# The first pair's rows as products with one-hot columns stationary, then turned like every other pair

## The chip, the cores and the metric

The kernel runs on 1 core of a Trainium2 chip. The metric is device time in microseconds (us), the median of several executions. In the trace and below, PE is TensorE (matrix products; PEld its loads of the stationary operand), DVE is VectorE, ACT is ScalarE, POOL is GpSimd and SP the engine that issues most transfers.

## What is computed

One step of a decoder trunk of two layers, on 512 prompt rows and 32 sample rows of width 1024, all float32. Each layer is a mixer (gated linear attention and a state-space scan in layer 0, pooling and block-sparse attention in layer 1), a residual with layer norm, a mixture of 32 experts (4 groups of 8, each row goes to one group and to two experts in it), and another residual with layer norm. The change lies between the first norm and the experts, in both layers:

```python
def _hier_moe(x, w_coarse, b_coarse, w_fine, b_fine, w_gate_up, w_down):
    xt = x.reshape(bsz * t, d)
    lc = xt @ w_coarse + b_coarse                    # 4 groups
    grp = argmax(lc); p_grp = softmax(lc)[grp]
    lf = einsum('nd,gde->nge', xt, w_fine) + b_fine  # 8 experts of each group
    top_v, top_i = lax.top_k(lf[grp], 2)
    gates = one_hot(top_i) * softmax(top_v) * p_grp
    for g in range(N_GROUPS):
        hg, hu = split(einsum('nd,edf->nef', xt, w_gate_up[g]), 2)
        out = out + einsum('nef,efd->nd', silu(hg) * hu * gate_g, w_down[g])
```

## The kernel before, in words

The 544 rows are five tiles in the order ORDER: the 32 sample rows first (i = 0), then four tiles of 128 prompt rows (i = 1 to 4). All five tiles stay on the chip in X.

A stage called settle (`settle_parts`) makes, tile by tile, the output projection of the mixer (`project`, L1378: products of 128x512 into the three banks `pp`, which are `ahead`), the residual and statistics (DVE, L1525 to L1530), the router's logits (`flip` L1394, `score` L1406) and the choice of experts (`choose`). The norm is applied to X by ACT (L1730) and then scale and bias by DVE (`affine`, L1564 and L1565), which says `final` when a tile is finished; SP then stores the tile to `token_rows` in memory (L1351).

The experts stage (`expert_parts`) goes through the 32 experts in 16 pairs. A pair takes 128 slots, 64 for each of its two experts. For pairs 1 to 15 POOL gathers the rows from `token_rows` into one of two tiles `xg` (L1279), PE turns them (`x_T`, 8 transposes, L1835), ACT and DVE copy them to `xT` (L1912), and then come `gate_up` in two halves (L1850), the hidden layer, and `down` (L1874). Rows over 64 for an expert go to extra pairs; one such pair runs in each layer.

The weights of a pair are 6 transfers of 1 MB: four for gate and up (`load_up`, L1254), two for down (`load_down`, L1260). They go round a ring of three places. Pairs 0 and 1 are loaded early. In `sync`, pair 2's four `up` transfers are issued after the last projection, then the store of the last tile, which waits for `final`, and then pair 2's two `down` transfers: the second of these overwrites `E.wd[-1]`, where the scale and bias (`gb`) lie until the last tile's `affine` is done. From pair 3 on, `Experts.load` waits for PE: the first half of `up` for the first half of gate_up three pairs back (`half_used`), the second half for its second half, `down` for the down products three pairs back. So pair 3's first transfers are released by the end of the first pair's gate_up, half 0 (L2005).

The first pair does not gather. DVE makes one-hot columns G (`heat`, L1621; 128 columns for each tile, which say what slot a row takes), and PE's `pick(i)` sums X-transposed times G over the five tiles straight into the turned form: 8 products for a tile, each with 128 columns of X (every eighth element of a row) stationary and 128 columns of G moving (L1436). ACT copies the sum to `xT` (L1734), and `first.gate_up` runs.

Beside it DVE works out where each row goes: `position` (L1611 to L1614) for a tile from PE's `count` (L1416), `start_of` (L1603), the tiles of an expert (L1659, from PE's `totals`, L1427), PE's prefix sums `placed` (L1477, L1479), and the chain from L1671 to the one-hots L1684 and L1687 (`destined`, `onehots`), from which PE makes the tables of rows (L1488, L1493).

Of the kernel before, what the change touches and what calls it, by code (L numbers as in the profile page):

```python
# [91 lines left out]
class Count:  # L92


    def __init__(self, eng, sem):
        self.eng, self.sem, self.n = eng, sem, 0
# [1129 lines left out]
class Experts:  # L1226
# [29 lines left out]

    def load_down(self, eng, i):
        for a in range(2):
            row = (self.l * NE + 2 * i + a) * 128
            eng.dma_start(self.wd[2 * (i % self.RING) + a][:, :], self.w_dn[row:row + 128, :])\  # L1260
               .then_inc(self.down_in[i % self.RING], 16)
# [22 lines left out]
def settle_parts(nc, s, place, C, X, lng, lnb, ln_T, mixT, w_dram, l, w_router, b_router, lg, xT, rows, E, back, done, ahead, first, old=None):  # L1284
# [24 lines left out]
    slots = place("slots", [128, 5, 2])  # L1309
    G = E.xg[0][:, 0:640].rearrange("p (t n) -> p t n", t=5)  # L1310

# [16 lines left out]
    x_in = [s.sem(f"x_in{i}") for i in range(5)]  # L1328
    hot, tables = s.sem("hot"), s.sem("tables")
    xt, x0, sl, hr = first.picked, first.x0, first.sl, first.hr  # L1330

    def sync(sp):
        sp.dma_start(wr[:, :, :], w_router[l]).then_inc(router_in, 16)
        sp.dma_start(gbT[:, :, :], ln_T).then_inc(router_in, 16)
        sp.dma_start(br[:, :], b_router[l].partition_broadcast(128)).then_inc(router_in, 16)
        if back:
            for i, (t, P) in enumerate(ORDER):
                sp.dma_start(X[:P, t, :], back(t)).then_inc(x_in[t], 16)
                if i == 0:
                    for p, got in ((slice(0, 32), old_in), (slice(32, 128), rest_in)):  # L1340
                        for a in range(2):
                            sp.dma_start(E.xg[a][p, :], old[a].partition_broadcast(p.stop - p.start)).then_inc(got, 16)
        sp.dma_start(gb[:, 0, :], lng.partition_broadcast(128)).then_inc(gb_in, 16)
        sp.dma_start(gb[:, 1, :], lnb.partition_broadcast(128)).then_inc(gb_in, 16)
        E.fill(sp, range(E.RING - 1))
        for i, (t, P) in enumerate(ORDER):
            if i == 4:
                sp.wait_ge(summed, 10)
                E.load_up(sp, E.RING - 1)
            sp.wait_ge(final, i + 1)  # L1350
            sp.dma_start(rows[tok0(t):tok0(t) + P, :], X[:P, t, :]).then_inc(stored, 16)  # L1351
        E.load_down(sp, E.RING - 1)

    def gpsimd(pool):
        if old:
            pool.wait_ge(old_used, 1)
        for x in E.xg:
            nc.gpsimd.memset(x[:, :], 0.0).then_inc(blank, 1)  # L1358
        pool.wait_ge(blank, 2)
        pool.wait_ge(told, 1)  # L1360
        pool.wait_ge(stored, 16 * 5)
        E.rows(pool, rows, 1, s.kept[f"e{l}_rows1"])
        pool.wait_ge(tables, 1)

    def tensor(pe):
# [57 lines left out]
        def totals():  # L1423
            pe.wait_ge(logit_c, 4)
            pe.wait_ge(assigned, 5)
            for i in range(5):
                last = nc.tensor.matmul(pm[1][0:32, 0:8], A12[:, i, :], C("ones")[:, 0:8], start=(i == 0), stop=(i == 4))  # L1427
            last.then_inc(counted, 1)

        def pick(i):  # L1430
            t, P = ORDER[i]
            pe.wait_ge(hot, i + 1)
            pe.wait_ge(final, i + 1)
            rows_of = X[:P, t, :].rearrange("r (p j) -> r j p", j=KD)
            for j in range(KD):
                last = nc.tensor.matmul(pt[j // 4][:, (j % 4) * 128:(j % 4) * 128 + 128], rows_of[:, j, :], G[:P, i, :],  # L1436
                                        start=(i == 0 and j % 4 == 0), stop=(i == 4), skip_group_check=True)
            if i == 4:
                last.then_inc(xt, 1)

# [5 lines left out]
        for i in range(1, 5):  # L1446
# [14 lines left out]
            if i < 4:  # L1461
# [9 lines left out]
        pick(0)  # L1471
        pick(1)
        totals()
        count(4)
        pick(2)
        pe.wait_ge(tiled, 1)
        nc.tensor.matmul(pm[0][:, 0:32], tilesT[:, 0:1].to_broadcast([32, 128]), C("before")[0:32, 0:32],  # L1477
                         start=True, stop=True)
        nc.tensor.matmul(pm[0][:, 32:64], tilesT[:, 0:1].to_broadcast([32, 128]), C("tri_p")[0:32, 0:32],  # L1479
                         start=True, stop=True).then_inc(placed, 1)  # L1480
        pick(3)
        pick(4)
        first.gate_up(pe, 0)
# [13 lines left out]
    def vector(dve):  # L1497
# [58 lines left out]

        def affine(i):
            t, P = ORDER[i]
            if i == 0:
                dve.wait_ge(gb_in, 32)  # L1560
            for h in range(2):
                x = X[:P, t, 512 * h:512 * h + 512]
                dve.wait_ge(normed, 2 * i + h + 1)
                c.step(V.tensor_tensor(x, x, gb[:P, 0, 512 * h:512 * h + 512], ALU.mult))  # L1564
                last = V.tensor_tensor(x, x, gb[:P, 1, 512 * h:512 * h + 512], ALU.add)  # L1565
            last.then_inc(final, 1)

# [49 lines left out]
        def heat(i):  # L1617
            dve.wait_ge(positioned, i + 1)
            if i == 0:
                dve.wait_ge(blank, 2)  # L1620
            V.tensor_tensor(G[:, i, :].rearrange("p (e n) -> p e n", e=2), slots[:, i, :].unsqueeze(2).to_broadcast([128, 2, 64]),  # L1621
                            C("iota")[:, 1:65].unsqueeze(1).to_broadcast([128, 2, 64]), ALU.is_equal).then_inc(hot, 1)
# [32 lines left out]
        position(3)  # L1655
        heat(3)
        start_of(4)
        dve.wait_ge(counted, 1)
        c.step(V.tensor_tensor(cmpT[:, :], pm[1][0:32, 0:8], C("m64")[0:32, :], ALU.is_gt))  # L1659
        V.tensor_reduce(tilesT[:, :], cmpT[:, :], AX.X, ALU.add).then_inc(tiled, 1)  # L1660
        position(4)
        heat(4)
        affine(4)
        c.wait()
        r10, b10 = rsel[:, :, :].rearrange("p k t -> p (k t)"), bsel[:, :, :].rearrange("p k t -> p (k t)")
# [53 lines left out]
    def scalar(act):  # L1719
        for i, (t, P) in enumerate(ORDER):  # L1720
# [7 lines left out]
            for h in range(2):  # L1728
                x = X[:P, t, 512 * h:512 * h + 512]
                nc.scalar.activation(x, x, ACT.Identity, bias=nmr[:P, t:t + 1], scale=rstd[:P, t:t + 1])\  # L1730
                  .then_inc(normed, 1)
        act.wait_ge(xt, 1)
        for h in range(2):
# [10 lines left out]
def expert_parts(nc, s, C, E, xT, xd, yd, first, px, py, Y, y_in):  # L1744
# [13 lines left out]
    all_landed = s.sem("all_landed")  # L1758
    xt, gh, gu, sl, hr = first.picked, first.gh, first.gu, first.sl, first.hr
    xta, xtd, ht, htc, dn, ya, ydv = (s.sem(x) for x in ("x_act", "x_dve", "h_T", "h_copied", "down", "y_act", "y_dve"))  # L1760
# [231 lines left out]
class FirstPair:  # L1992


    def __init__(self, nc, se, E, xT, pg, ph):
        self.nc, self.E, self.xT, self.pg, self.ph = nc, E, xT, pg, ph
        self.picked, self.x0, self.gh, self.gu, self.sl, self.hr = (se.sem(x) for x in (
            "x_T", "x_first", "gate_up_half", "gate_up", "silu", "hidden"))

    def gate_up(self, pe, h):  # L2000
# [18 lines left out]
def settle_and_experts(nc, l, C, X, lng, lnb, ln_T, mixT, w_dram, w_router, b_router, lg, xT, xd, yd, E, back, done, ahead, old, y_in):  # L2019


    with Scope(nc, f"n{l}0") as s, Scope(nc, f"e{l}") as se:
# [13 lines left out]

        first = FirstPair(nc, se, E, xT, ahead[0:2], ahead[2])
        (sync1, pool1, pe1, dve1, act1), px, py = settle_parts(nc, s, place, C, X, lng, lnb, ln_T, mixT, w_dram, l, w_router,
# [915 lines left out]
```

## Time and profile before

| | us |
|---|---|
| three runs | 1339.84, 1342.57, 1347.92 |
| median | 1342.57 |
| time of the profiled execution | 1343.1 |
| its span | 1341.2 |
| mean granted TensorE clock | 0.922 |
| PE busy | 1139.0 (85%) |
| DVE busy | 488.2 (36%) |
| ACT busy | 253.7 (19%) |
| memory traffic, mean over the span | 279 GB/s |

The time holds 1.9 us more than the span (1343.1 - 1341.2), which lie around the program. A product of float32 stands in the trace as two records, with two loads of the stationary operand; a transpose stands as one. PEclk is the granted clock as a share of 2.4 GHz: 1.00 is 2.4 GHz, 0.50 is 1.2 GHz, a value between is a stretch with both.

### The profile page before, as it was taken

How to read it: one execution, taken by the hardware profiler on the slowest of the kernel's cores; microseconds unless marked ns; L12 is line 12 of the kernel's file. 1: busy time of each engine (PE TensorE's matmuls, PEld its weight loads, DVE VectorE, ACT ScalarE, POOL GpSimd, SP SyncE). 2: the span in 40 equal slices, each digit the busy share in tenths (PEclk: the TensorE clock that was granted, in tenths of full speed). 3: DMA queues.
4: the chain of work that ended last, by engine and by line, in shares of the span. 5: the costliest groups of instructions: out<-in, count | busy, mean ns of one | idle time of the engine just before them, and what ended most of it. 6: DMA issues, size and time to landing. Idle time of an engine off the chain costs nothing. (4 is left out here: it accounts for less than half of the span.)

```text
span 1341.2 us, 15442 instructions
## 1 busy us (share of the span) xinstructions
PE 1139.0 (85%) x5825; PEld 591.5 (44%) x5825; DVE 488.2 (36%) x1338; ACT 253.7 (19%) x548; POOL 186.0 (14%) x182
## 2 busy tenths in 40 slices
PE   7999999969999977884689998987999999778552
PEld 5874666635753322221334345544457433223110
DVE  2614755556631111113411324654775211111008
ACT  0311222411111111112411213241111111111011
POOL 0000000000011111102533542220000211111112
PEclk9999998989889988897789999998998999889885
DMA  7430301173369999995866998793916999999914
GB/s 266 159 107 1 130 1 63 72 286 162 155 259 413 419 421 420 420 386 199 318 205 244 396 360 323 304 342 106 420 50 228 358 418 419 421 420 421 387 66 159
DMA packets 84453, 358.90 MB, mean 268 GB/s; under 512 B 13828, under 2 KB 18053, under 8 KB 54422
## 3 DMA queue, kind: packets, MB, share of 16 engines
q1 hardware_dynamic: 62774, 279.63, 52.7%
q0 software_dynamic: 19520, 74.01, 14.4%
q10 hardware_dynamic: 2080, 4.19, 0.8%
q8 instruction: 50, 0.82, 0.2%
q14 instruction: 29, 0.24, 0.0%
HBM read 342.82 MB, written 31.16 MB: 279 GB/s over the span
## 5 line engine op out<-in xcount | busy, mean ns | idle before, releaser
L1850 PE MATMUL ahead_psum<-m_wg,top_xT 128*64 128x512 f32 x672 | 165.6, 641 | 44.6 <-DMA m_wg<-in_moe_w_gate_up 43.6
L1874 PE MATMUL n_psum_m<-m_wd,top_xT 128*64 128x512 f32 x528 | 123.9, 612 | 5.5 <-DMA m_wd<-in_moe_w_down 3.4
L1378 PE MATMUL ahead_psum<-top_wide,top_xT 128*128 128x512 f32 x240 | 112.4, 616 | 8.6 <-DVE top_X L1527 8.6
L1850 PEld LDWEIGHTS ahead_psum<-m_wg,top_xT 128*64 128x64 f32 x672 | 50.8, 147 | 152.7 <-issue 98.3
L1850 PE MATMUL ahead_psum<-top_wide,top_xT 128*64 128x512 f32 x320 | 80.1, 648 | 19.9 <-DMA top_wide<-in_moe_w_gate_up 19.9
L1912 DVE COPY top_xT<-n_psum_t 128x512 f32<-128x512 f32 x31 | 21.4, 692 | 188.3 <-PE n_psum_t L1835 188.3
L2251 PE MATMUL cd_psum_ab<-top_wide,top_xT 128*128 128x512 f32 x192 | 87.9, 611 | 0.1
L1279 POOL DMA_INDIRECT m_xg<-token_rows,m_tokof x31 | 31.5, 1018 | 373.8 <-PE n_psum_t L1835 198.7
L1921 DVE TENSOR_SCALAR e_Y<-n_psum_m,m_share 128x512 f32<-128x512 f32 x33 | 24.8, 751 | 129.7 <-PE n_psum_m L1874 129.7
L2095 POOL DMA_INDIRECT cd_kv<-in_cache_kT,top_kpages x64 | 60.6, 947 | 78.8 <-PE cd_psum_d L2293 51.0
L1378 PEld LDWEIGHTS ahead_psum<-top_wide,top_xT 128*128 128x128 f32 x240 | 45.3, 197 | 57.4 <-issue 57.3
L1874 PEld LDWEIGHTS n_psum_m<-m_wd,top_xT 128*64 128x64 f32 x528 | 36.3, 140 | 68.7 <-issue 61.3
L1783 POOL DMA_INDIRECT expert_rows<-e_Y,m_dest x33 | 32.7, 992 | 188.1 <-DVE e_Y L1921 187.2
L2251 PEld LDWEIGHTS cd_psum_ab<-top_wide,top_xT 128*128 128x128 f32 x192 | 36.5, 195 | 49.1 <-issue 49.0
L588 PE MATMUL ab_psum<-top_wide,top_xT 128*128 128x512 f32 x128 | 56.9, 597 | 0.0
L1850 PEld LDWEIGHTS ahead_psum<-top_wide,top_xT 128*64 128x64 f32 x320 | 24.3, 148 | 73.1 <-issue 47.9
L1358 POOL MEMSET m_xg<- 128x1024 f32 x4 | 3.7, 949 | 380.5 <-POOLq L144 275.2
L1965 DVE TENSOR_TENSOR top_xT<-top_xT,ahead_psum 128x256 f32<-128x256 f32 x31 | 13.1, 421 | 103.4 <-ACT top_xT L1934 103.4
L1929 ACT ACTIVATE top_xT<-ahead_psum 128x256 f32<-128x256 f32 x33 | 12.6, 383 | 193.5 <-PE ahead_psum L1861 193.5
L1920 ACT ACTIVATE e_Y<-n_psum_m,m_share 128x512 f32<-128x512 f32 x33 | 22.7, 687 | 109.1 <-PE n_psum_m L1874 109.1
L2104 POOL DMA_INDIRECT cd_kv<-in_cache_v,top_pages x32 | 30.1, 940 | 78.9 <-PE cd_psum_e L2334 62.6
L1436 PE MATMUL n_psum_t<-m_xg,top_X 128*128 128x128 f32 (+1 forms) x160 | 40.4, 430 | 0.0
(488 smaller groups left out, 1668.4 us busy)
## 6 DMA issues: line engine op xcount, KB each, us to landing
m_wg<-in_moe_w_gate_up SPq DMA_DIRECT2D x88, 1024.0 KB, 26.3
m_wd<-in_moe_w_down SPq DMA_DIRECT2D x64, 1024.0 KB
top_wide<-in_moe_w_gate_up SPq DMA_DIRECT2D x40, 1024.0 KB, 25.4
cd_kv<-in_cache_kT SPq DMA_DIRECT2D x64, 256.0 KB
m_wg<-expert_rows SPq DMA_DIRECT2D x16, 512.0 KB, 5.8
ab_w<-in_ab_w_in SPq DMA_DIRECT2D x2, 2048.0 KB, 11.7
top_wide<-in_ab_w_in SPq DMA_DIRECT2D x2, 2048.0 KB, 7.7
top_wide<-in_ab_w_out SPq DMA_DIRECT2D x2, 2048.0 KB, 8.6
```

The lines of the kernel that those rows point to most:

```text
L588: last = mm(out[:, :], xT[:, k, tok0(t):tok0(t) + 128], w[i][:, k, :], start=(k == 0), stop=(k == KD - 1))
L1279: pool.indirect_dma_start(out=self.xg[i % 2][:, :], out_offset=None, in_=xd, in_offset=bass.IndirectOffsetOnAxis(ap=self.tokof[:, i:i + 1] ...
L1378: last = nc.tensor.matmul(pp[(2 * i + h) % 3][:P, :], mixT[:, k, tok0(t):tok0(t) + P], w[h][:, k, :], start=(k == 0), stop=(k == KD - 1))
L1436: last = nc.tensor.matmul(pt[j // 4][:, (j % 4) * 128:(j % 4) * 128 + 128], rows_of[:, j, :], G[:P, i, :], start=(i == 0 and j % 4 == 0), ...
L1783: nc.gpsimd.indirect_dma_start(out=yd, in_=Y[i % 2][:, :], in_offset=None, out_offset=bass.IndirectOffsetOnAxis(ap=E.dest[:, i:i + 1], axi ...
L1850: last = nc.tensor.matmul(pg[i % 2][64 * a:64 * a + 64, :], xgT[i % 2][:, j, 64 * a:64 * a + 64], wg[2 * (i % NR) + a][:, j * 512:(j + 1) ...
L1874: last = nc.tensor.matmul(py[n2][64 * a:64 * a + 64, :], hT[:, j, 64 * a:64 * a + 64], wd[2 * (i % NR) + a][:, j * D + n2 * 512:j * D + (n ...
L1920: ins = nc.scalar.activation(dst, py[half][:, :], ACT.Copy, scale=share) if half == 0 else \
L1921: nc.vector.tensor_scalar(dst, py[half][:, :], share, None, ALU.mult)
L2095: pool.indirect_dma_start(out=self.slots[slot][:, b, 512 * j:512 * j + 512], out_offset=None, in_=self.k_rows, in_offset=bass.IndirectOffs ...
L2104: pool.indirect_dma_start(out=self.slots[slot][:, b, :], out_offset=None, in_=self.v_rows, in_offset=bass.IndirectOffsetOnAxis(ap=self.pag ...
L2251: last = nc.tensor.matmul(out[:, :], xT[:, k, tok0(t):tok0(t) + 128], w[r][:, k, :], start=(k == 0), stop=(k == KD - 1))
```

## The change

`pick` makes, for each tile, two products of 128x512 with G stationary and X moving, into the banks `pp[1]` and `pp[2]`: the first pair's rows as plain rows. ACT copies these to `xg[0]`, and 8 transposes (`first.x_T`) turn them, as for other pairs. G moves to `xg[1]`, and only `xg[1]` is blanked by POOL. The last tile's `affine` is done in halves with `position(4)` and `heat(4)` between them, `final` counts halves, `start_of(4)` and L1659 stand behind the second half, and PE's `count(4)` stands ahead of `totals`, and `placed` behind the last `pick`. One of pair 2's two `down` transfers is issued ahead of the last tile's store.

```diff
-    def load_down(self, eng, i):
-        for a in range(2):
+    def load_down(self, eng, i, experts=(0, 1)):
+        for a in experts:
@@
-    G = E.xg[0][:, 0:640].rearrange("p (t n) -> p t n", t=5)
+    G = E.xg[1][:, 0:640].rearrange("p (t n) -> p t n", t=5)
@@ sync
                 E.load_up(sp, E.RING - 1)
-            sp.wait_ge(final, i + 1)
+                E.load_down(sp, E.RING - 1, (0,))
+            sp.wait_ge(final, 2 * i + 2)
             sp.dma_start(rows[tok0(t):tok0(t) + P, :], X[:P, t, :]).then_inc(stored, 16)
-        E.load_down(sp, E.RING - 1)
+        E.load_down(sp, E.RING - 1, (1,))
@@ gpsimd
-        for x in E.xg:
-            nc.gpsimd.memset(x[:, :], 0.0).then_inc(blank, 1)
-        pool.wait_ge(blank, 2)
+        nc.gpsimd.memset(E.xg[1][:, :], 0.0).then_inc(blank, 1)
         pool.wait_ge(told, 1)
         pool.wait_ge(stored, 16 * 5)
+        pool.wait_ge(xt, 1)
         E.rows(pool, rows, 1, s.kept[f"e{l}_rows1"])
@@ tensor
         def pick(i):
             t, P = ORDER[i]
             pe.wait_ge(hot, i + 1)
-            pe.wait_ge(final, i + 1)
-            rows_of = X[:P, t, :].rearrange("r (p j) -> r j p", j=KD)
-            for j in range(KD):
-                last = nc.tensor.matmul(pt[j // 4][:, (j % 4) * 128:(j % 4) * 128 + 128], rows_of[:, j, :], G[:P, i, :],
-                                        start=(i == 0 and j % 4 == 0), stop=(i == 4), skip_group_check=True)
-            if i == 4:
-                last.then_inc(xt, 1)
+            for h in range(2):
+                pe.wait_ge(final, 2 * i + h + 1)
+                last = nc.tensor.matmul(pp[1 + h][:, :], G[:P, i, :], X[:P, t, 512 * h:512 * h + 512], start=(i == 0), stop=(i == 4))
+                if i == 4:
+                    last.then_inc(picked, 1)
@@
         pick(0)
         pick(1)
+        count(4)
         totals()
-        count(4)
         pick(2)
+        pick(3)
+        pick(4)
         pe.wait_ge(tiled, 1)
...
-        pick(3)
-        pick(4)
+        first.x_T(pe, rows_out, pt)
         first.gate_up(pe, 0)
@@ vector
-        def affine(i):
+        def affine(i, halves=(0, 1)):
...
-            for h in range(2):
+            for h in halves:
...
-                last = V.tensor_tensor(x, x, gb[:P, 1, 512 * h:512 * h + 512], ALU.add)
-            last.then_inc(final, 1)
+                V.tensor_tensor(x, x, gb[:P, 1, 512 * h:512 * h + 512], ALU.add).then_inc(final, 1)
@@
         heat(3)
+        affine(4, (0,))
+        position(4)
+        heat(4)
+        affine(4, (1,))
+        c.wait()
         start_of(4)
         dve.wait_ge(counted, 1)
...
-        position(4)
-        heat(4)
-        affine(4)
-        c.wait()
+        dve.wait_ge(positioned, 5)
@@ scalar
+        for h in range(2):
+            act.wait_ge(picked, h + 1)
+            nc.scalar.activation(E.xg[0][:, 512 * h:512 * h + 512], pp[1 + h][:, :], ACT.Copy).then_inc(rows_out, 1)
         act.wait_ge(xt, 1)
@@ class FirstPair
+    def x_T(self, pe, rows_out, px):
+        pe.wait_ge(rows_out, 2)
+        xv = self.E.xg[0][:, :].rearrange("r (p j) -> r j p", j=KD)
+        for j in range(KD):
+            last = self.nc.tensor.transpose(px[j // 4][:, (j % 4) * 128:(j % 4) * 128 + 128], xv[:, j, :], self.C("ident"))
+        last.then_inc(self.turned, 1)
```

PE, layer 0, from the last logits to the first pair's gate_up, before (the row of one program line with its count; L1436 is `pick`, L2005 gate_up):

```order
L1406 MATMUL n_psum_m<-e_Y,top_xT 128x36 x4
L1436 MATMUL n_psum_t<-m_xg,top_X 128x128 x16
L1427 MATMUL n_psum_m<-top_consts,e_Y 32x8 x5
L1416 MATMUL n_psum_r<-e_Y,top_consts 128x32
L1436 MATMUL n_psum_t<-m_xg,top_X 128x128 x8
L1477 MATMUL n_psum_m<-top_consts,e_Y 128x32
L1479 MATMUL n_psum_m<-top_consts,e_Y 128x32
L1436 MATMUL n_psum_t<-m_xg,top_X 128x128 x16
L2005 MATMUL ahead_psum<-m_wg,top_xT 64x512 x8
```

The same place in the changed kernel (L1435 is `pick`, L2007 the transposes of `first.x_T`, L2015 gate_up):

```order
L1406 MATMUL n_psum_m<-e_Y,top_xT 128x36 x4
L1435 MATMUL ahead_psum<-top_X,m_xg 128x512 x4
L1416 MATMUL n_psum_r<-e_Y,top_consts 128x32
L1427 MATMUL n_psum_m<-top_consts,e_Y 32x8 x5
L1435 MATMUL ahead_psum<-top_X,m_xg 128x512 x6
L1477 MATMUL n_psum_m<-top_consts,e_Y 128x32
L1479 MATMUL n_psum_m<-top_consts,e_Y 128x32
L2007 MATMUL n_psum_t<-top_consts,m_xg 128x128 x8
L2015 MATMUL ahead_psum<-m_wg,top_xT 64x512 x8
```

40 products of 128 columns became 10 of 512, `placed` (L1477, L1479) moved behind all of them, and 8 transposes came in between.

DVE, layer 0, behind `heat(3)` (the first row), before (L1564, L1565 are `affine`, L1603 `start_of`, L1611 `position`, L1666 the next chain):

```order
L1621 TENSOR_TENSOR m_xg<-e_Y,top_consts 128x128
L1603 TENSOR_TENSOR e_Y<-e_Y,top_consts 128x64
L1604 TENSOR_REDUCE e_Y<-e_Y 128x2
L1659 TENSOR_TENSOR e_Y<-n_psum_m,top_consts 32x8
L1660 TENSOR_REDUCE e_Y<-e_Y 32x1
L1611 TENSOR_TENSOR e_Y<-e_Y,n_psum_r 128x64
L1613 TENSOR_REDUCE e_Y<-e_Y 128x2
L1614 SCALAR_TENSOR_TENSOR e_Y<-n_psum_r,e_Y 128x2
L1621 TENSOR_TENSOR m_xg<-e_Y,top_consts 128x128
L1564 TENSOR_TENSOR top_X<-top_X,m_wd 128x512
L1565 TENSOR_TENSOR top_X<-top_X,m_wd 128x512
```

And now (L1563 and L1564 are `affine`, L1601 `start_of`, L1609 `position`, L1619 `heat`):

```order
L1619 TENSOR_TENSOR m_xg<-e_Y,top_consts 128x128
L1563 TENSOR_TENSOR top_X<-top_X,m_wd 128x512
L1564 TENSOR_TENSOR top_X<-top_X,m_wd 128x512
L1609 TENSOR_TENSOR e_Y<-e_Y,n_psum_r 128x64
L1611 TENSOR_REDUCE e_Y<-e_Y 128x2
L1612 SCALAR_TENSOR_TENSOR e_Y<-n_psum_r,e_Y 128x2
L1619 TENSOR_TENSOR m_xg<-e_Y,top_consts 128x128
L1563 TENSOR_TENSOR top_X<-top_X,m_wd 128x512
L1564 TENSOR_TENSOR top_X<-top_X,m_wd 128x512
L1601 TENSOR_TENSOR e_Y<-e_Y,top_consts 128x64
L1602 TENSOR_REDUCE e_Y<-e_Y 128x2
L1662 TENSOR_TENSOR e_Y<-n_psum_m,top_consts 32x8
```

The first half of the last tile's scale and bias moved ahead of its one-hot, and the count of tiles (now L1662) behind the second half.

## Rows read from the trace of the kernel before

**Rows 1.** The page: busy share of the DMA engines in 40 slices of the span

```profile
DMA  7430301173369999995866998793916999999914
```

**Rows 2.** Windows, layer 0: length, PE, PEld, DVE, ACT, POOL busy, PEclk, DMA share, GB/s

```profile
350.60:362.00 11.40, 10.31 (x49) 9.71 (x50) 6.80 (x32) 2.21 (x4) 0.00 (x0) 0.74 0.92 357
362.00:367.00 5.00, 5.00 (x29) 4.86 (x28) 3.88 (x13) 0.00 (x0) 0.00 (x0) 0.58 0.07 30
367.00:372.40 5.40, 5.40 (x25) 5.36 (x25) 4.70 (x14) 0.00 (x0) 0.00 (x0) 0.75 0.88 326
372.40:381.60 9.20, 8.42 (x31) 4.74 (x29) 1.20 (x9) 3.88 (x5) 0.00 (x0) 0.78 0.22 94
381.60:402.00 20.40, 20.12 (x110) 11.05 (x112) 6.52 (x21) 2.65 (x5) 3.16 (x3) 0.92 0.86 313
402.00:420.00 18.00, 18.00 (x89) 6.45 (x85) 2.29 (x4) 2.43 (x5) 4.00 (x4) 1.00 1.01 402
```

**Rows 3.** What SP issues in layer 0: start, length of the issuing, line

```profile
350.62 2.01 SPq L1254 DMA_DIRECT2D top_wide<-in_moe_w_gate_up  x4
...
367.18 1.26 SPq L1260 DMA_DIRECT2D m_wd<-in_moe_w_down  x2
381.62 6.74 SPq L1254 DMA_DIRECT2D m_wg<-in_moe_w_gate_up  x4
```

**Rows 4.** PE in order of time, layer 0: start, length, records, idle before

```profile
336.38 3.60 PE L1378 MATMUL ahead_psum<-top_wide,top_xT 128*128 128x512 f32 x8
...
353.73 8.29 PE L1436 MATMUL n_psum_t<-m_xg,top_X 32*128 32x128 f32 x32
...
363.03 4.04 PE L1436 MATMUL n_psum_t<-m_xg,top_X 128*128 128x128 f32 x16
...
367.56 7.90 PE L1436 MATMUL n_psum_t<-m_xg,top_X 128*128 128x128 f32 x32
376.24 5.35 PE L2005 MATMUL ahead_psum<-m_wg,top_xT 128*64 128x512 f32 x16 [0.78 <-ACT top_xT L1734]
381.52 2.41 PE L1488 MATMUL n_psum_m<-top_xT 128*128 128x24 f32 x20
...
390.77 1.97 PE L1835 MATMUL n_psum_t<-top_consts,m_xg 128*128 128x128 f32 x8
```

**Rows 5.** PE in order of time, layer 1

```profile
1010.28 8.19 PE L1436 MATMUL n_psum_t<-m_xg,top_X 32*128 32x128 f32 x32
...
1019.06 4.05 PE L1436 MATMUL n_psum_t<-m_xg,top_X 128*128 128x128 f32 x16
...
1032.27 3.65 PE L2005 MATMUL ahead_psum<-m_wg,top_xT 128*64 128x512 f32 x16 [0.78 <-ACT top_xT L1734]
1035.86 2.41 PE L1488 MATMUL n_psum_m<-top_xT 128*128 128x24 f32 x20
...
1063.14 1.06 PE L1835 MATMUL n_psum_t<-top_consts,m_xg 128*128 128x128 f32 x8
```

**Rows 6.** Loads of the stationary operand, and a product, by line: ns least/median/greatest

```profile
L1378 PEld LDWEIGHTS ahead_psum<-top_wide,top_xT x240: 186/190/337, 282.9 to 1005.9; 128*128 128x128 f32 x120
L1378 PE MATMUL ahead_psum<-top_wide,top_xT x240: 592/592/1192, 282.9 to 1006.3; 128*128 128x512 f32 x120
L1436 PEld LDWEIGHTS n_psum_t<-m_xg,top_X x160: 307/335/338, 353.7 to 1031.0; 128*128 128x128 f32 x128, 32*128 32x128 f32 x32
```

**Rows 7.** DVE in order of time, layer 0

```profile
358.24 0.29 DVE L1621 TENSOR_TENSOR m_xg<-e_Y,top_consts 128x128 f32<-128x128 f32 x1
...
364.04 0.69 DVE L1564 TENSOR_TENSOR top_X<-top_X,m_wd 128x512 f32<-128x512 f32 x1
...
367.74 0.19 DVE L1671 TENSOR_SCALAR e_Y<-n_psum_m 128x32 f32<-128x32 f32 x1 [0.40 <-PE n_psum_m L1479]
...
372.29 0.42 DVE L1687 TENSOR_TENSOR top_xT<-e_Y,top_consts 128x256 f32<-128x256 f32 x1
```

**Rows 8.** ACT in order of time, layer 0

```profile
375.49 1.09 ACT L1734 ACTIVATE top_xT<-n_psum_t 128x512 f32<-128x512 f32 x2 [20.74 <-PE n_psum_t L1436]
```

More of the change, by code:

```diff
@@ L1328, in settle_parts @@
     x_in = [s.sem(f"x_in{i}") for i in range(5)]
-    hot, tables = s.sem("hot"), s.sem("tables")
-    xt, x0, sl, hr = first.picked, first.x0, first.sl, first.hr
+    hot, tables, picked, rows_out = (s.sem(x) for x in ("hot", "tables", "picked", "rows_out"))
+    xt, x0, sl, hr = first.turned, first.x0, first.sl, first.hr
     def sync(sp):
@@ L1619, in heat @@
             if i == 0:
-                dve.wait_ge(blank, 2)
+                dve.wait_ge(blank, 1)
             V.tensor_tensor(G[:, i, :].rearrange("p (e n) -> p e n", e=2), slots[:, i, :].unsqueeze(2).to_broadcast([128, 2, 64]),
@@ L1758, in expert_parts @@
     all_landed = s.sem("all_landed")
-    xt, gh, gu, sl, hr = first.picked, first.gh, first.gu, first.sl, first.hr
+    xt, gh, gu, sl, hr = first.turned, first.gh, first.gu, first.sl, first.hr
     xta, xtd, ht, htc, dn, ya, ydv = (s.sem(x) for x in ("x_act", "x_dve", "h_T", "h_copied", "down", "y_act", "y_dve"))
@@ L1992, with __init__ @@
 class FirstPair:
-    def __init__(self, nc, se, E, xT, pg, ph):
-        self.nc, self.E, self.xT, self.pg, self.ph = nc, E, xT, pg, ph
-        self.picked, self.x0, self.gh, self.gu, self.sl, self.hr = (se.sem(x) for x in (
+    def __init__(self, nc, se, C, E, xT, pg, ph):
+        self.nc, self.C, self.E, self.xT, self.pg, self.ph = nc, C, E, xT, pg, ph
+        self.turned, self.x0, self.gh, self.gu, self.sl, self.hr = (se.sem(x) for x in (
             "x_T", "x_first", "gate_up_half", "gate_up", "silu", "hidden"))
+    def x_T(self, pe, rows_out, px):
[4 more added lines that the diff above has]
+        last.then_inc(self.turned, 1)
     def gate_up(self, pe, h):
@@ L2035, in place @@
             return v
-        first = FirstPair(nc, se, E, xT, ahead[0:2], ahead[2])
+        first = FirstPair(nc, se, C, E, xT, ahead[0:2], ahead[2])
         (sync1, pool1, pe1, dve1, act1), px, py = settle_parts(nc, s, place, C, X, lng, lnb, ln_T, mixT, w_dram, l, w_router,
```

## The prediction

> **What bounds the kernel now.** I read the page first, for where the memory is busy. The row of the DMA engines has two long stretches of 9s, slices 13 to 18 and 32 to 37: there the experts' weights stream in, and ahead of each is a weaker stretch [rows 1]. Then the windows of layer 0 say what goes on at that edge. From 402 us on the DMA engines are full (share 1.01) and nothing PE does can shorten the stream; but from 362 to 367 us their share is 0.07, from 372.4 to 381.6 us 0.22, and from 381.6 to 402 us 0.86, while PE is busy nearly all the time [rows 2]. So the stream's end is set by when it starts and by how much idle time lies in front of it. What starts it is the row of SP: after pair 2's loads (350.62 and 367.18 us) nothing is issued until 381.62 us [rows 3], and that is 0.1 us behind the start of PE's L1488 at 381.52 us, that is, the end of the first pair's gate_up, half 0 [rows 4]. PE sets it: `pick` runs from 353.73 us, gate_up begins at 376.24 us [rows 4]. Layer 1 is the same, with pick from 1010.28, gate_up from 1032.27 and its end at 1035.86 us [rows 5]. The question is how much earlier gate_up's half 0 ends.
>
> **What the old pick costs.** 8.29 us for two tiles, 4.04 for one, 7.90 for two: 20.2 us a layer [rows 4]. A tile has 16 records, so 253 ns for each; the load of the stationary operand is 335 ns in the middle (every eighth element of a row), where projections with contiguous columns have 190 ns [rows 6], and PEld is busy 4.86 of the 5.00 us from 362 to 367 [rows 2]. So loads bound it. That a tile took 4.04 us in a stretch at mean clock 0.58 and 3.95 at 0.75 [rows 2, 4] agrees.
>
> **What the new one costs.** A tile is two products of 128x512 with contiguous columns of G stationary. The nearest row is the projection: 8 records, 4 products, in 3.60 us [rows 4]. The last record lasts 592 ns to its end [rows 6], the other seven start (3.60-0.59)/7 = 0.43 us apart, so a product in a chain costs 0.86 us; 3.60/4 = 0.90 is the upper end. Ten make 8.6 us (to 9.0). The 592 ns are the same under all records but the slow ones, and a slow record takes up to 1192 [rows 6].
>
> **The new chain to gate_up, layer 0.** Picks 0 and 1 start at 353.73 and take 3.44, to 357.17. `count(4)` then waits for `position(3)`, just ahead of the one-hot of tile 3 at 358.24 [rows 7]; so it starts at 358.25, a wait of 1.1 that the old picks hid. `count` and `totals` take 0.6 (1010.28 + 8.19 to 1019.06 in layer 1 [rows 5]): 358.85. Picks 2 to 4, 5.16: 364.0. Does DVE keep up? Behind 358.24+0.29 it has now half an `affine` (two of 0.69 [rows 7], ACT's norm being done at 375.49-20.74 = 354.75, when its idle time began [rows 8]), position and one-hot of tile 4 (0.8, from the same pattern ahead of 364.04), and the second half: hot 5 at about 360.7, the last `final` at 362.0, the tile count at 362.9. Pick 4 starts at 362.3, its second product at 363.1: none of these is late, the nearest with 1 us in hand. `placed` takes 0.7 until DVE goes on (0.6 on PE); DVE resumes at 364.7, where it was 367.74 [rows 7].
>
> The relay is what the change adds on this path. ACT's copy of half 0 lies under the last product. That of half 1 starts some 0.2 behind it, at 364.2, and takes 0.6 (two of 128x512 from PSUM take 1.09, the second overlapping [rows 8]): 364.8. PE starts the transposes at 364.95. Eight cost 1.06 at full clock [rows 5] and 1.97 in the row at 390.77 [rows 4]; I take 1.06, since all that precedes is dense 512-column work like the projection. From the last transpose to gate_up there are two halves of the same ACT copy, of which the first is waited for, 0.78 as now [rows 4]. Gate_up starts at 366.8, 9.4 us before 376.24. It took 5.35 in layer 0 and 3.65 in layer 1 [rows 4, 5]: the first at a mixed clock (0.78 from 372.4 to 381.6 [rows 2]) after 22 us of load-bound picks. Behind dense products I expect 3.65. Then half 0 ends at 370.4, where it was 381.52: **11.1 us**. With the old 5.35 it would be 9.4.
>
> **Layer 1.** Its pick starts 656.55 us behind layer 0's, and what precedes is the same, so gate_up starts at 1023.35, 8.9 before 1032.27, and with 3.65 as before ends 8.9 us earlier: **8.9 us** [rows 5].
>
> On the transposes the Trainium skill speaks otherwise: "TensorE: Matmul & The Clock Gate", Part 4, says that the full clock does not engage for transposes. The trace differs: eight took 1.06 us in the stretches at 1.00 [rows 2, 5]. By that page they would take 1.97, and the sum would be 1.8 us less, 1325.
>
> **What else moves, and its cover.** PE's L1488 waits for `destined` and the one-hots. They ended at 372.71 [rows 7], 8.8 us ahead; the DVE chain moves only 3.0 us, to 369.7, so the cover shrinks to 0.7 us in each layer. If DVE is later than I have it, L1488 and all behind it (half 1, and the gather of pair 1) wait for the excess. The waits for the ring: pair 2's loads begin at 350.62 as before. Six of 1.05 MB at the 402 GB/s of 402 to 420 us [rows 2] take 15.6 us, the store of half a MB 1.3, so they are in by 368, ahead of 370.4. The `down` half that is issued early fills the idle stretch from 362 us; the other half waits behind the last store, now at 362.0 instead of 366.8. It is costed at nothing, as is the later store behind 1 MB, since the gather needs it only after the tables (L1488 plus 3 us). Without the early half the loads would end near 368 all the same; the cost would still be nothing. Bounds: 0 to 1 us. One blanking less on POOL and the gather's wait for the transposes (366 us, gather wanted at 374): nothing, in both directions. The old stores and copies need nothing else.
>
> **Can the stream use the whole gain?** Idle DMA time between 350.6 and 402 is 0.9+4.7+0.6+7.2+2.9 = 16.3 us [rows 2], more than 11.1. Behind the release the chain (gate_up 1, tables, gather, down of pair 0) keeps its order and lengths, so the 2.9 us there stay, and the full stretch starts and ends earlier by the same amount. What follows the experts waits for them.
>
> **Sum.** 11.1 + 8.9 = 20.0 us. Against the profiled execution's 1343.1 that is **1323.1 us**; the median is 0.5 lower than it, so I say 1323.
>
> **Rivals.**
> (1) *DVE sets the tables.* If the split `affine` and waits leave the one-hots 3 us behind my 369.7, 2.3 us a layer are lost for all but the first release: 1323 + 4.6 = 1328. For it: the cover is 0.7. Against: every DVE term is a measured row.
> (2) *Picks at the lower clock.* Stretches around the old picks are at 0.58 to 0.78 [rows 2]. If the new ones run at 1.2 GHz, each product takes 1.71 (twice 0.86, for it would be bound by columns): 8.6 more, less the 1.1 wait that they would fill, 7.5 a layer: 1338, no change that can be told. Against: the projection of the same form ran at 0.86 just before, and picks follow it with 512 columns, not 128.
> (3) *Slower: the lower clock holds from the picks to the end of gate_up's half 1.* Full-clock work of 8.6 + 1.0 + 3.6 + 3.6 = 16.8 a layer runs twice as long, less 1.1: 15.7, in both 31.4 against the gain of 20.0: 1354. It decides once more than 20 us of such work in both layers are at 1.2 GHz. For it: two waits for ACT of 0.4 and 0.8 us stand ahead of gate_up; against: the old chain had the second of these and layer 1 ran 3.65 behind it.
> (4) *The change doesn't do what it says:* a product with G and X stays as slow as a tile of 4.04 for a reason that is not the load. Then picks end at 375, the relay of 2.8 comes on top, gate_up starts 1.6 to 2 us later than before: 1343 to 1347. Against: 335 ns against 190 [rows 6].
>
> On the loads, the same page (LDWEIGHTS, "loading the stationary operand") gives a time that goes by columns, 107 ns for 128, whatever the rows. By that, an estimate, 16 loads would be 1.7 us, the load would not be what the old tile's 4.04 came from, and rival 4 would hold. The trace differs, with 335 and 190 ns for 128 columns each, and the measurement decides.
>
> **How the numbers follow.** Forecast 0.75, rival 1 0.12, rival 2 0.06, rival 3 0.03, rival 4 0.04. The forecast's own spread: layer 0's and 1's gate_up at a mixed clock, +1.7 each, transposes at 1.97, +1.8, products at 0.90, +0.8, loads late, +1: to 1330. Downward, what follows (transposes of pair 1 at 390.77 took 1.97, also slow) may gain 1 to 3 us from a better clock: 1320. The three runs of before lie from 2.7 below to 5.4 above their median, so a median of the new can be off by 2 to 4. With rival 1 inside, the range is 1317 to 1333. It leaves rivals 2 to 4 out. A median of this kernel tells 0.5% (6.7 us) from no change: faster than that is forecast and rival 1, 0.87; within it rivals 2 and 4, 0.09; slower 0.04 (rival 3 and a bad end of 4).
>
> **What would show it.** Right: L1435 in 4 and 6 products at 0.86 each; a wait of about 1 us ahead of L1416; ACT's L1734 in the place given and L2007 about 1 us long; gate_up from 366.8 and, in layer 1, from 1023.35-11.1 = 1012.3, SP's releases at 370.5 and 1015.9; DMA share over 0.5 in the stretch 370 to 380. Wrong: PEclk near 0.5 during L1435 or L2015, PE waiting for L1684 or L1687 ahead of L1487, PE waiting for DMA in the first gate_ups, or a stream whose first full stretch starts earlier while its end stays.

## The result

The changed kernel took 1327.57 us (median of 4 runs, 1320.55 to 1333.42) where the kernel before, in 4 runs, took 1341.20: a ratio of 0.9892, 95% interval 0.9859 to 0.9924. In a second series it was 0.9869 (0.9844 to 0.9894). So it is 1.1 to 1.3% faster, some 14 to 18 us. The forecast was 1323 in a range of 1317 to 1333: the direction and the mechanism held, and the gain was 12 to 32% smaller than the 20.0 us forecast. The profiled execution of the changed kernel is its slowest of the first series, 1333.42 us; its span is 1331.6.

PE in order of time in layer 0 of the changed kernel (start, length, records):

```profile
354.46 6.18 PE L1435 MATMUL ahead_psum<-top_X,m_xg 32*128 32x512 f32 x8
360.43 0.47 PE L1416 MATMUL n_psum_r<-e_Y,top_consts 128*128 128x32 f32 x2
360.84 0.70 PE L1427 MATMUL n_psum_m<-top_consts,e_Y 128*32 128x8 f32 x10
361.47 7.68 PE L1435 MATMUL ahead_psum<-top_X,m_xg 128*128 128x512 f32 x12
...
369.84 1.16 PE L2007 MATMUL n_psum_t<-top_consts,m_xg 128*128 128x128 f32 x8
371.78 3.65 PE L2015 MATMUL ahead_psum<-m_wg,top_xT 128*64 128x512 f32 x16 [0.78 <-ACT top_xT L1737]
375.36 2.41 PE L1487 MATMUL n_psum_m<-top_xT 128*128 128x24 f32 x20
```

and in layer 1:

```profile
1006.39 6.17 PE L1435 MATMUL ahead_psum<-top_X,m_xg 32*128 32x512 f32 x8
...
1013.39 7.69 PE L1435 MATMUL ahead_psum<-top_X,m_xg 128*128 128x512 f32 x12
...
1023.71 3.65 PE L2015 MATMUL ahead_psum<-m_wg,top_xT 128*64 128x512 f32 x16 [0.78 <-ACT top_xT L1737]
1027.29 2.41 PE L1487 MATMUL n_psum_m<-top_xT 128*128 128x24 f32 x20
```

I count the stretch from the start of the first pick to the start of the tables' products (L1488 before, L1487 now), which start 0.1 us ahead of the release of pair 3's loads, and call it the chain. The release in layer 0, SP's row:

```profile
375.46 6.74 SPq L1254 DMA_DIRECT2D m_wg<-in_moe_w_gate_up  x4
```

The chain was 27.8 us in layer 0 and 25.6 in layer 1 [rows 4, 5]; it is 20.9 in both now. That is 6.9 and 4.7 us less, 11.6 together, where 20.0 were forecast. One thing in the chain is far from the forecast: the ten products take 6.0 + 7.6 us instead of 3.4 + 5.2. That hides the wait of 1.1 us that was forecast ahead of L1416, and `count` and `totals` take 1.0 instead of 0.6; the rest has the length of the forecast. The clock says why. Windows of the changed kernel, layer 0 (columns as in [rows 2]):

```profile
350.00:354.40 4.40, 3.30 (x20) 2.12 (x18) 2.38 (x7) 1.12 (x3) 0.00 (x0) 1.00 0.46 127
354.40:357.00 2.60, 2.60 (x7) 0.82 (x6) 2.05 (x12) 1.09 (x2) 0.00 (x0) 0.77 1.01 419
357.00:360.40 3.40, 3.40 (x4) 1.37 (x5) 3.12 (x14) 0.00 (x0) 0.00 (x0) 0.50 1.01 422
360.40:363.00 2.60, 2.60 (x15) 1.79 (x14) 2.14 (x7) 0.00 (x0) 0.00 (x0) 0.50 1.02 429
363.00:366.00 3.00, 3.00 (x5) 1.11 (x4) 1.29 (x9) 0.00 (x0) 0.00 (x0) 0.50 0.98 406
366.00:369.00 3.00, 3.00 (x8) 1.12 (x6) 0.00 (x0) 0.60 (x1) 0.00 (x0) 0.99 1.04 425
369.00:371.80 2.80, 1.89 (x15) 1.54 (x14) 1.81 (x6) 1.36 (x3) 0.00 (x0) 1.00 0.13 56
371.80:375.40 3.60, 3.60 (x17) 1.25 (x17) 3.43 (x13) 1.60 (x2) 0.00 (x0) 1.00 0.00 0
```

From about 356 to 366 us the granted clock was 1.2 GHz, as it was at the same place before [rows 2], only that there the picks did not feel it. It is full again for the transposes and gate_up, so layer 0's gate_up took the 3.65 us of the forecast, against 5.35 in the profile of the kernel before. The DMA engines, idle for some 7 us ahead of the old release (0.78 of 9.2 us [rows 2]), are still idle for 6.

### The profile page after: what moved, and what is told of

The parts are those of the page before. It is cut to its first block and busy times, and to the rows that moved or that the text cites. A ratio compares the mean times of both kernels' runs of the same rounds, so it can differ in the third digit from the quotient of the medians.

```text
span 1331.6 us, 15236 instructions
## 1 busy us (share of the span) xinstructions
PE 1131.4 (85%) x5721; PEld 566.9 (43%) x5721; DVE 487.7 (37%) x1338; ACT 256.3 (19%) x552; POOL 187.5 (14%) x180
## 5 line engine op out<-in xcount | busy, mean ns | idle before, releaser
L2261 PE MATMUL cd_psum_ab<-top_wide,top_xT 128*128 128x512 f32 x192 | 85.2, 597 | 0.0
L1723 ACT ACTIVATE top_xT<-n_psum_t 128x512 f32<-128x512 f32 (+1 forms) x20 | 10.2, 532 | 140.9 <-PE n_psum_t L1394 140.9
## 6 DMA issues: line engine op xcount, KB each, us to landing
top_wide<-in_moe_w_gate_up SPq DMA_DIRECT2D x40, 1024.0 KB, 24.3
```

The source lines that it names most:

```text
L2261: last = nc.tensor.matmul(out[:, :], xT[:, k, tok0(t):tok0(t) + 128], w[r][:, k, :], start=(k == 0), stop=(k == KD - 1))
```

## The experiments

Each kernel was timed in a series beside the kernel before, on the same chip. Ratios are to that. The series are three: one with `fill`, `fill_pick2`, `form_only` and `order_only`, one with `delay`, `down_late`, `before_contig` and `before_fill`, and one with the changed kernel again, both `fill` kernels again and `wait_more`. Only the last of them has the changed kernel in it.

**One part of the change at a time.** `form_only` undoes all of the change but the new picks, the copy and the transposes, and what these need (G's new place, the one blanking, `final` in halves):

```diff
@@ vector
         heat(3)
-        affine(4, (0,))
-        position(4)
-        heat(4)
-        affine(4, (1,))
-        c.wait()
         start_of(4)
...
+        position(4)
+        heat(4)
+        affine(4)
+        c.wait()
@@ tensor
-        count(4)
         totals()
+        count(4)
         pick(2)
-        pick(3)
-        pick(4)
         pe.wait_ge(tiled, 1)
...
+        pick(3)
+        pick(4)
@@ sync
-                E.load_down(sp, E.RING - 1, (0,))
...
-        E.load_down(sp, E.RING - 1, (1,))
+        E.load_down(sp, E.RING - 1)
```

> The new form of the picks with copy and transposes, but the old order on DVE and PE (scale and bias of the last tile behind its one-hot and in one piece, totals ahead of count(4), placed ahead of pick 3) and both down transfers behind the last store. If the new form alone carries the gain: 21 to 22 us from first pick to release, 1327 to 1330. If the last tile's scale and bias must come earlier for it to pay: DVE ends them some 3 us later than in the changed kernel, at 12.8 us behind the first pick instead of 8.7, and with picks 3 and 4 then done by 14 to 15 us nothing waits for more than 0.5 us at the low clock; so I expect at most 1 us a layer lost, under 1330.

It took 1326.17 us, ratio 0.9864 (0.9831 to 0.9897): all of the gain, as far as these intervals can tell. Its chains were 18.5 and 20.0 us, shorter than the 21 to 22 that I expected, because the clock fell for a shorter time. The wait that I expected to be under 0.5 us is 0.69: PE waits so long for ACT's second copy, since `placed` no longer fills that gap.

`order_only` is the other half: the new order, the split scale and bias, and the early down transfer, with the old picks.

```diff
-            for h in range(2):
-                pe.wait_ge(final, 2 * i + h + 1)
-                last = nc.tensor.matmul(pp[1 + h][:, :], G[:P, i, :], X[:P, t, 512 * h:512 * h + 512], ...)
...
+            pe.wait_ge(final, 2 * i + 2)
+            rows_of = X[:P, t, :].rearrange("r (p j) -> r j p", j=KD)
+            for j in range(KD):
+                last = nc.tensor.matmul(pt[j // 4][...], rows_of[:, j, :], G[:P, i, :], ...)
...
-        first.x_T(pe, rows_out, pt)
@@ scalar
-        for h in range(2):
-            act.wait_ge(picked, h + 1)
-            nc.scalar.activation(E.xg[0][:, 512 * h:512 * h + 512], pp[1 + h][:, :], ACT.Copy).then_inc(rows_out, 1)
```

> The old form of the picks (8 products with strided X stationary for a tile, straight into the turned form, no copy and no extra transposes) with the new order, the split scale and bias and the early down transfer. Theory: the loads of X bound the picks, so the new order gives nothing: 20.2 us of picks a layer, 25.7 to 27.9 us from first pick to release as before, 1340 to 1342. If the order carries part of the gain, it would be below 1337.

1340.44 us, ratio 0.9986 (0.9962 to 1.0011), chains 26.2 and 26.2, the release here 0.9 us ahead of the tables. The time shows no gain, and there is a flaw that the changed kernel barely avoids: with `placed` behind all picks DVE's one-hots are late, and the tables wait for them. PE in layer 0 of `order_only`:

```profile
374.52 3.65 PE L2013 MATMUL ahead_psum<-m_wg,top_xT 128*64 128x512 f32 x16 [0.22 <-ACT top_xT L1735]
379.10 2.41 PE L1488 MATMUL n_psum_m<-top_xT 128*128 128x24 f32 x20 [0.92 <-DVE top_xT L1687]
```

In the changed kernel the last one-hot ends at 374.79, 0.6 us ahead of the tables at 375.36; the forecast had this cover at 0.7. DVE, layer 0 of the changed kernel:

```profile
374.37 0.42 DVE L1687 TENSOR_TENSOR top_xT<-e_Y,top_consts 128x256 f32<-128x256 f32 x1
```

`down_late` issues both down transfers behind the last store, as before:

```diff
-                E.load_down(sp, E.RING - 1, (0,))
...
-        E.load_down(sp, E.RING - 1, (1,))
+        E.load_down(sp, E.RING - 1)
```

> The changed kernel with both down transfers of pair 2 behind the last store, as before the change. Theory: nothing, since the memory is idle in 363 to 375 us anyway and pair 2's down products come late: 1327.6 within what can be told, the release at 21.0 us behind the first pick. Rival: the early half takes idle time out ahead of the release, and without it pair 3's loads start behind a queue: 1 to 2.5 us a layer slower.

1330.49 us, ratio 0.9891 (0.9859 to 0.9924), as the changed kernel within what can be told; a few microseconds either way can't be excluded. In layer 0 its DMA engines ran dry (share under 0.1) from 369.6 us, only 0.4 us ahead of the release at 370.02, so an earlier release would have met pair 2's loads still coming in. It gave more than was asked: in its layer 0 the clock stayed up, and the chain is there to be seen as the forecast had it. PE, layer 0 of `down_late` (L1434 is `pick`, L2014 gate_up, L1486 the tables):

```profile
352.96 3.89 PE L1434 MATMUL ahead_psum<-top_X,m_xg 32*128 32x512 f32 x8
357.57 0.38 PE L1415 MATMUL n_psum_r<-e_Y,top_consts 128*128 128x32 f32 x2 [0.72 <-DVE e_Y L1611]
357.88 0.48 PE L1426 MATMUL n_psum_m<-top_consts,e_Y 128*32 128x8 f32 x10
358.30 5.42 PE L1434 MATMUL ahead_psum<-top_X,m_xg 128*128 128x512 f32 x12
...
366.34 3.65 PE L2014 MATMUL ahead_psum<-m_wg,top_xT 128*64 128x512 f32 x16 [0.78 <-ACT top_xT L1736]
369.92 2.41 PE L1486 MATMUL n_psum_m<-top_xT 128*128 128x24 f32 x20
```

with this window, granted clock 1.00:

```profile
353.00:362.00 9.00, 8.28 (x30) 3.77 (x30) 8.07 (x37) 0.98 (x2) 0.00 (x0) 1.00 0.96 401
```

That is 17.0 us of chain, where the forecast had 370.4 - 353.7 = 16.7. Layer 1 of the same execution had a clock of 0.61 in the first 8.4 us behind the first pick, and a chain of 19.2.

**Why the old picks were slow.** `before_contig` is the kernel before with contiguous columns of X as the stationary operand. It changes which features stand where in the first pair's turned rows, so that they meet the wrong rows of the weights; all lengths are otherwise comparable.

```diff
-            rows_of = X[:P, t, :].rearrange("r (p j) -> r j p", j=KD)
+            rows_of = X[:P, t, :].rearrange("r (j p) -> r j p", j=KD)
```

> The kernel before, with pick taking 128 contiguous elements of each row as the stationary operand instead of every eighth (the first pair's features then stand in another order, so its expert products are of mismatched features). Theory: the stride makes the load slow; loads fall from 335 to about 190 ns and a tile from 4.04 to 3.0 to 3.4 us, five tiles from 20.2 to 15 to 17. Rival: the load's length doesn't depend on the stride, or it isn't what bounds the tile: 20 us of picks as before and 1341.

The theory held, and the picks gained more than it said. The loads and products of the picks, by line:

```profile
L1436 PEld LDWEIGHTS n_psum_t<-m_xg,top_X x160: 181/192/333, 350.5 to 1016.0; 128*128 128x128 f32 x128, 32*128 32x128 f32 x32
L1436 PE MATMUL n_psum_t<-m_xg,top_X x160: 270/275/582, 350.5 to 1016.1; 128*128 128x128 f32 x128, 32*128 32x128 f32 x32
```

192 ns against 335 [rows 6], and a tile of 2.03 us against 4.04, five tiles 9.9 us in layer 0. The kernel took 1329.12 us in 4 runs, ratio 0.9892 (0.983 to 0.9953). That is a gain of the size of the whole change's, from the stride alone, and the layer 0 chain, 15.6 us at full clock, is 1.4 us shorter than the changed kernel's 17.0, since there is no copy and no second turning. In layer 1 the clock fell and a tile took up to 3.76 us, so this form too feels the clock once the loads are no longer what bounds it.

**The clock.** Two theories for the stretch at 1.2 GHz: (A) the waits and small products of PE ahead of the picks bring it down; (B) it falls by chance whatever PE did there. `fill` puts products into an idle bank in those waits:

```diff
         project(4, 1, second[2:])
+        idle_products(nc, C, pp[1], 2)
         flip(4, 1)
         pe.wait_ge(added, 8)
         count(3)
+        idle_products(nc, C, pp[1], 1)
         score(4, 1)
```

> The changed kernel with three products into an idle bank in the waits ahead of the picks: two of 256 columns between the last projection and the last tile's transposes, one ahead of the last logits. Theory A (the clock fell to 1.2 GHz because PE had waits and small products in the 4 us ahead of the picks): granted clock 1.00 from the picks on, each product 0.86 us instead of up to 1.72, a wait of about 1 us ahead of L1416 comes up, from the first pick to the release of pair 3's loads 17.1 us a layer instead of 21.0, the kernel 7 us faster than the changed one: about 1320. Theory B (the picks themselves, or something that waits have no part in, bring the clock down): clock 0.50 over some 10 us as before, 21.0 us a layer, time up by at most 0.6: about 1328.

> The kernel of fill. Theory A: again under 3.5 us at 1.2 GHz in a layer, 17.0 to 17.6 us from first pick to L1489, and 4 to 8 us faster than the changed kernel on the same chip. Theory B (the clock falls by chance and the earlier good passes were luck): 3 to 10 us at 1.2 GHz in one of the two layers, and no difference from the changed kernel beyond 2 us.

In the first series 1319.47 us, ratio 0.9833 (0.9803 to 0.9863), in the second 1329.01, 0.9875 (0.9846 to 0.9905). `fill_pick2` also lets pick 2 fill the wait ahead of `count(4)`:

```diff
         pick(1)
+        pick(2)
         count(4)
         totals()
-        pick(2)
```

> As fill, and PE's pick(2) ahead of count(4), so that the 1.1 us in which PE waits for position(3) hold products. Theory A: 16.1 us from the first pick to the release, 2 us in all below fill: about 1318. Theory B: there is no wait to fill, the same as fill, 1328.

> The kernel of fill_pick2. Theory A: full clock in the picks of both layers, 16.0 us from first pick to L1489, 5 to 10 us faster than the changed kernel on the same chip. Theory B: the clock falls in one of the layers, and it is within 3 us of the changed kernel.

1323.41, ratio 0.9840 (0.9808 to 0.9872), and 1324.92, 0.9841 (0.9816 to 0.9865). Layer 0 of `fill_pick2` from first pick to tables, 16.0 us at a clock of 1.00:

```profile
352.30:362.00 9.70, 9.70 (x33) 4.29 (x32) 8.52 (x39) 1.61 (x3) 0.00 (x0) 1.00 1.02 426
362.00:368.30 6.30, 5.39 (x30) 2.75 (x29) 5.21 (x18) 2.97 (x4) 0.00 (x0) 1.00 0.85 332
```

`wait_more` goes the other way:

```diff
         score(4, 1)
+        pe.wait_ge(normed, 10)
         pick(0)
```

> The changed kernel with PE waiting ahead of the first pick until ACT's norm of the last tile is done, 1.0 to 1.1 us more of idle PE. Theory A: the clock falls in both layers for 7 to 10 us; 21 to 22 us from first pick to L1487 counted from the old moment, 2 to 6 us slower than the changed kernel. Theory B: at full clock the wait at L1416 shrinks by as much, so nothing is lost but 0 to 1 us a layer, and the clock is no worse than in the changed kernel.

1335.83 us, ratio 0.9922 (0.9897 to 0.9948), in the series in which the changed kernel had 0.9869: 0.5% slower, some 7 us, for 0.9 to 1.0 us of wait in a layer. Layer 1:

```profile
1007.65 7.49 PE L1435 MATMUL ahead_psum<-top_X,m_xg 32*128 32x512 f32 x8 [0.87 <-ACT top_X L1731]
```

```profile
1007.60:1018.00 10.40, 10.35 (x23) 4.62 (x24) 7.15 (x30) 0.00 (x0) 0.00 (x0) 0.50 0.92 391
```

The changed kernel itself, again:

> The changed kernel itself, for two more passes of its clock and for times on the same chip as the next three. Theory A (waits and small products ahead of the picks bring the clock down, at a moment that chance shifts): in each layer 3 to 10 us at 1.2 GHz or, by chance, none; from first pick to L1487 17 to 21 us; 1325 to 1330. Theory B (chance alone): the same.

1326.98 us, ratio 0.9869; chains 17.6 and 19.3. `before_fill` is the kernel before with the three filling products:

> The kernel before, with the same three idle products ahead of the picks. If the clock is what matters for the old picks too: under 18 us of picks. Theory: they are bound by loads, a tile stays 4.04 us at either clock; the low clock then still comes, since PE's products are a small part of each tile: 1341, within 2 us.

1343.07 us, ratio 0.9984 (0.9956 to 1.0013), and picks of 8.29, 4.04 and 7.90 us in layer 0, as before. But filling did not keep the clock up here: it fell under the old picks all the same, so this run alone does not show that the clock doesn't matter to them. Two stretches with the tile of 4 us in them show it, layer 0 of `before_fill` (4.04 us) and then layer 1 of the kernel before (4.05 us [rows 5]):

```profile
364.90:368.90 4.00, 4.00 (x18) 3.88 (x18) 3.67 (x12) 0.00 (x0) 0.00 (x0) 0.53 0.01 4
```

```profile
1018.30:1023.00 4.70, 4.70 (x30) 4.49 (x28) 3.80 (x13) 0.00 (x0) 0.00 (x0) 1.00 0.06 26
```

A tile took as long at a clock of 0.53 as at 1.00.

The chains of all profiled executions, each the start of the tables' first product less the start of the first pick (us):

| kernel | layer 0 | layer 1 |
|---|---|---|
| before | 27.8 | 25.6 |
| before_fill | 26.1 | 26.2 |
| order_only (release 0.9 sooner) | 26.2 | 26.2 |
| before_contig | 15.6 | 20.0 |
| changed | 20.9 | 20.9 |
| changed, again | 17.6 | 19.3 |
| down_late | 17.0 | 19.2 |
| delay (with 5.0 us of added work) | 22.0 | 24.3 |
| form_only | 18.5 | 20.0 |
| wait_more | 20.9 | 21.9 |
| fill | 17.6 | 17.0 |
| fill, again | 17.6 | 17.0 |
| fill_pick2 | 16.0 | 16.0 |
| fill_pick2, again | 17.7 | 16.0 |

The changed kernel's picks in unchanged surroundings (changed twice, down_late, and delay less its 5.0 us: 8 passes, a pass being one layer of one execution) lie 0 to 3.9 us above the 17.0 of full clock, 1.9 in the mean. With filled waits (8 passes) it is 0 to 1.7 above the full-clock chain (17.0, or 16.0 with pick 2 moved), 0.4 in the mean. With a longer wait both passes are 4 to 5 above.

The two layers differ, and this is the better evidence. In layer 1, where PE waits 1.05 us ahead of L1394, the clock fell in all five executions whose PE work ahead of the picks is that of the changed kernel (changed twice, `down_late`, `delay`, `form_only`), and in none of the four with filled waits; chance alone would split nine passes so once in 126. In layer 0, where that wait is 0.78 us, it fell in three of five, and in three of four with filling: no difference that can be told. There was a share of DMA traffic near 1.0 during the picks whether the clock fell or not (1.01 and 1.02 in the windows of the changed kernel, 1.02 in that of `fill_pick2`), so this doesn't decide it. So the traces speak for (A) in layer 1 and leave chance a good part in layer 0. The expectations for the second series came out mixed: `fill` had the chains of (A) but was 2 us slower than the changed kernel, where (A) had it 4 to 8 faster, and `fill_pick2` lost its clock in layer 0 and was 2 us faster, which is what (B) had.

The times follow less clearly. `wait_more` and the changed kernel have intervals that don't meet, in one series. `fill_pick2` is 0.5 and 0.3% below the changed kernel's ratio, but the first two come from different series, and the intervals overlap (0.9816 to 0.9865 against 0.9844 to 0.9894 in the second); `fill` alone was the fastest in one series and level with the changed kernel in the other. So that a longer wait costs is shown in the times, that filling gains only in the traces. `fill_pick2` is 1.6% faster than the kernel before, and in the series that has both its median is 2 us under the changed kernel's, which these runs can't tell from none.

**Does the end move one for one?** `delay` puts work of known length ahead of the transposes:

```diff
+        idle_products(nc, C, pp[0], 12)
         first.x_T(pe, rows_out, pt)
```

> The changed kernel with 12 products of 256 columns into an idle bank ahead of the first pair's transposes, at full clock 12 x 0.43 = 5.2 us a layer, less 0.4 that the wait for the copy covers: 4.8 a layer. Theory: whatever the release of pair 3's loads moves, the end moves one for one, so 9.6 us slower than the changed kernel, about 1337. Rival: the stream of weights takes part of a shift up in its idle stretches, so that a shift of 4.8 moves the end by 2.5 or less a layer: 1332 or less.

1337.97 us, ratio 0.993 (0.9904 to 0.9955), with `down_late` in the same series at 0.9891: 5 us by the ratios and 7.5 by the medians, for 4.9 to 5.0 us of delay in each layer (chain 21.95 in layer 0, at a clock of 1.00 like the 17.0 of `down_late`). That lies between the theory's 9.6 and the rival's 5, and the intervals hold both. The traces help: from the release to SP's first load of the combined rows (L181), layer 0 took 238.2 to 241.3 us in the five executions that released at 375 us or later (the kernel before with 239.4 among them), mean 239.8; in the nine that released earlier, at 366 to 372, it took 240.2 to 242.8, mean 241.6. In layer 1 it was 262.9 to 268.4 with no such order. So in layer 0 up to 2 us of what the release gained seem to be given back in the experts stage, and in layer 1 nothing that can be told from the scatter. It is not clean: the three lowest are also the three with the old picks, and the changed kernel's own 241.3 stands among the late ones. What takes these 2 us stays open.

## Why the prediction was right, and where its size came from

**The bound.** Right. The first pair's gate_up sets when pair 3's loads go out; the release came 0.1 us behind the start of the tables' products in every run but `order_only`'s, where these waited for DVE, and the kernel got faster by roughly what the chains got shorter (9.6 us of span for 11.6 of chains in the first profile, 18.9 for 16.5 in the second).

**The old picks are bound by strided loads.** Right, and the strongest result: `before_contig` halves them with nothing else changed, and a tile of the old picks took 4.04 us at a clock of 0.53 and 4.05 at 1.00. Of the page of the Trainium skill, "TensorE: Matmul & The Clock Gate", the section "LDWEIGHTS (loading the stationary operand)" has the time go by columns alone: the same 128 columns took 335 ns at a stride of eight elements and 192 contiguous. The trace doesn't agree with it. Rival 4, which hung on this, is out.

**The new picks at 0.86 us, ten for 8.6.** The step that was mis-sized. At full clock it holds within some tenths: 3.89 us for four and 5.42 for six, each with the last one's tail, and a chain of 17.0 where the forecast had 16.7. But the clock fell in six of the eight passes, and the ten took up to 13.6 us. The forecast reasoned that dense products would hold the clock. They don't decide it: in the first profile the fall comes some 1.4 us after the first pick starts (a mean of 0.77 over 354.4 to 357), and in the other passes between 0.2 us ahead of that start and 2.5 us behind it. What lies ahead of it is PE's waits of 0.78 and 0.32 us (1.05 and 0.32 in layer 1) and products of 32 and 36 columns. This is rival 2, which was given 0.06, in part: it cost 3.9 us in each layer of one execution, and 0.6 and 2.3, 0 and 2.2, 0 and 2.4 in the others. Its full price was 7.5 a layer. With 0.3 + 1.9 us a layer in the mean, 20.0 becomes 15.6, and with up to 2 us given back in layer 0 it is 13.6; measured by the ratios were 14 and 18.

**Layer 0's 11.1 us.** 1.7 of them were gate_up going from 5.35 to 3.65. The 5.35 rests on the one profile of the kernel before: in `before_fill` and `order_only`, which have the old picks too, gate_up took 3.65 in layer 0, and the chain was 26.1 and 26.2 instead of 27.8. So part of this term was the clock of one execution, which the change need not have brought, and how often the kernel before loses it stays open. Without it the sum above would be 14.0, or 12.0 with 2 us given back, against 14 and 18 measured: it meets the measured gain only roughly.

**The relay.** Right: ACT's second copy, 1.16 us of transposes with their tail, 0.78 to gate_up. The transposes took 1.04 to 1.16 us in every pass, in windows at 1.00, so the 1.97 us at the lower clock did not come up. The Trainium skill's "TensorE: Matmul & The Clock Gate", Part 4, says that the full clock does not engage for transposes; the trace differs from that page. The clock was already up when they began, and no run here shows what a longer stretch of them would do.

**DVE keeps up.** Right, with 0.6 us of cover. DVE was not late in any run with the new picks, and `order_only` shows the rival's wait, 0.92 us, where the picks end later than it.

**The early down transfer and the new order at nothing.** Nothing speaks against it for the transfer (`down_late`), to within the interval of its time; right for the order with the old picks, and `form_only` shows that the new picks don't need it either.

**The stream uses the whole gain.** Nearly: up to 2 us in layer 0 may be given back, which `delay` neither shows nor excludes.

**Slower (rival 3).** Not seen. gate_up ran at full clock in every pass of the new picks, even in `wait_more`.

## What to carry to other kernels

Where a matrix is to be multiplied by one-hots, look at which operand is stationary and with what stride it is read: here the load of strided columns, not the arithmetic, was the cost, and it can be seen as PEld busy nearly all through (4.86 of 5.00 us) and a length that the clock doesn't change (4.04 and 4.05 us at 0.53 and 1.00). Such a piece hides the clock; once it is mended, the clock becomes a term of its own, so price the products that follow at both levels when what precedes them is a patchwork of waits and small products, and see whether work of one's own (here a pick) can fill the waits. A term read from one profile can hold that execution's clock (here gate_up's 5.35 us): read it in a second one. A chain that releases a long stream of transfers is worth shortening even while the memory is the bound of the stage.

## What the hardware did that I had not expected

- A stationary operand of 128 float32 columns with a stride of 8 elements: 335 ns for a load, contiguous 192 ns, in the same instruction of the same program.
- The granted clock stood at 0.50 for 10 us in the middle of 128x512 products that followed each other without a gap, and rose again in the middle of them; in layer 0 of `down_late`, with the same instructions on PE, it stayed at 1.00.
- 0.9 to 1.0 us of additional wait ahead of such a stretch cost some 7 us in a kernel with two of them, and its chains were 5.9 us longer in sum than those of the changed kernel in the same series.
- With the waits ahead of it filled, the clock stayed up through the picks of layer 1 in four executions of four; unfilled, it fell there in five of five.
